# A hybrid attention encoder layer on one core: the projection's work on ScalarE and VectorE in another order, and GpSimd for part of the weight sums

## The reference, cut to what matters

```
h = rmsnorm(x, g_norm_mix)
qa, ka, va, qb, kb, vb = split(h @ w_in)
qb, kb = partial_rope(qb), partial_rope(kb)       # first 16 of 64 values of a head
oa = neighbourhood_attention(qa, ka, va, rpb); ob = windowed_gqa_sink(qb, kb, vb, sink)
x = x + concat(rmsnorm(oa), rmsnorm(ob)) @ w_out
x = x + (silu(n @ w_gate) * (n @ w_up)) @ w_down   # n = rmsnorm(x)
return rmsnorm(x, g_final)
```

## Time and profile before

| | us |
|---|---|
| median of 3 runs (lowest, highest) | 2266.8 (2265.73, 2267.71) |
| the profiled execution's own time | 2267.85 |
| its span, first to last instruction | 2266.0 |
| values phase, 12.1 to 146.7 | 134.6 |
| products, 146.7 to 462.2 | 315.5 |
| last product to the seventeenth score | 36.9 |
| the rest (attention, mix, FFN) | 1766.9 |

### The profile page before, as it was taken

The page is one execution under the profiler, slowest core; times in us unless marked ns, Lnnn a source line. Parts: engine busy times, 40 slices in busy tenths (PEclk is TensorE's granted clock), DMA queues, the critical chain, the costliest instruction groups (busy, mean ns, idle before and its releaser), DMA issues.

```text
span 2266.0 us, 33068 instructions
## 1 busy us (share of the span) xinstructions
PE 2166.6 (96%) x11168; PEld 1787.7 (79%) x11168; DVE 1565.9 (69%) x2892; ACT 1012.7 (45%) x1967; POOL 243.7 (11%) x275
## 2 busy tenths in 40 slices
PE   7888988969999999999999999999999999999998
PEld 5677766758888888888888888888888888888887
DVE  5466676649988868777666666866666678665676
ACT  5443443448889944344333334433333334131333
POOL 2234100036400000001211111100000000000000
PEclk9989998989999999999999999999999999999999
DMA  6666676899985356665555557623232276353544
GB/s 196 186 192 196 194 243 225 276 246 259 243 219 172 110 190 211 241 219 171 190 172 190 172 190 251 222 89 121 89 121 89 103 287 235 112 181 110 178 152 157
DMA packets 267558, 419.34 MB, mean 185 GB/s; under 512 B 15242, under 2 KB 157074, under 8 KB 260896
## 3 DMA queue, kind: packets, MB, share of 16 engines
q1 hardware_dynamic: 254736, 378.20, 52.2%
q0 software_dynamic: 10240, 30.48, 4.5%
q10 hardware_dynamic: 2448, 8.91, 1.3%
HBM read 264.70 MB, written 156.04 MB: 186 GB/s over the span
## 4 chain that ended last, share of the span: by engine, by line
PE 80%; DVE 7%; DMA 5%; issue 3%; ACT 3%; SPq 1%; DVEq 0%; ACTq 0%
PE late_psum L2334 11%; PE late_psum L2336 11%; PE late_psum L2335 11%; PE late_psum L2360 6%; PE late_psum L2361 6%; PE late_psum L2362 6%; PE late_psum L1278 4%; PE late_psum L1255 3%; PE late_psum L1676 3%; PE late_psum L1678 3%; PE late_psum L1677 3%; PE late_psum L853 2%; PE late_psum L855 2%; PE late_psum L854 2%; PE late_psum L1243 2%
## 5 line engine op out<-in xcount | busy, mean ns | idle before, releaser
L2334 PE MATMUL late_psum<-ff_h,ff_ring 128*128 128x512 f32 x1232 | 479.6, 389 | 1.3 <-DVE ff_acts L2195 1.2
L2336 PE MATMUL late_psum<-ff_h,ff_ring 128*128 128x512 f32 x1232 | 479.3, 389 | 0.0
L2335 PE MATMUL late_psum<-ff_h,ff_ring 128*128 128x512 f32 x1232 | 479.3, 389 | 0.0
L2334 PEld LDWEIGHTS late_psum<-ff_h,ff_ring 128*128 128x128 f32 x1232 | 231.2, 188 | 50.1 <-DVE ff_acts L2195 2.1
L2335 PEld LDWEIGHTS late_psum<-ff_h,ff_ring 128*128 128x128 f32 x1232 | 231.2, 188 | 48.0
L2336 PEld LDWEIGHTS late_psum<-ff_h,ff_ring 128*128 128x128 f32 x1232 | 231.2, 188 | 47.9
L2360 PE MATMUL late_psum<-ff_d,ff_a 128*128 128x512 f32 x616 | 240.1, 390 | 2.1 <-DVE ff_x L2253 1.4
L2362 PE MATMUL late_psum<-ff_d,ff_a 128*128 128x512 f32 x616 | 239.7, 389 | 0.0
L2361 PE MATMUL late_psum<-ff_d,ff_a 128*128 128x512 f32 x616 | 239.7, 389 | 0.0
L2253 DVE TENSOR_TENSOR ff_x<-late_psum,ff_x 128x512 f32<-128x512 f32 x224 | 153.3, 689 | 118.1 <-PE late_psum L2362 117.5
L2153 DVE TENSOR_TENSOR ff_ring<-ff_raw,ff_ring 128x512 fp32r<-128x512 f32 x176 | 130.1, 740 | 101.2 <-ACT ff_ring L2030 101.2
(11 more groups left out here) (204 smaller groups left out, 4125.8 us busy)
## 6 DMA issues: line engine op xcount, KB each, us to landing
acts_scratch<-ff_acts SPq DMA_DIRECT2D x22, 1792.0 KB, 7.5
ff_a<-acts_scratch SPq DMA_DIRECT2D x24, 960.0 KB, 5.3
ff_raw<-in_w_gate SPq DMA_DIRECT2D x44, 512.0 KB, 3.8
ff_raw<-in_w_up SPq DMA_DIRECT2D x44, 512.0 KB, 3.9
att_q_stack<-qk_scratch SPq DMA_DIRECT2D x64, 256.0 KB, 6.5
ff_d<-down_scratch SPq DMA_DIRECT2D x21, 768.0 KB, 6.8
...
```

The lines of the kernel that those rows point to most:

```text
L2334: pe.matmul(out_bank, whi[:, k], hhi[:, :, k], start=(k == 0 and not onto), stop=False, skip_group_check=onto)
L2335: pe.matmul(out_bank, whi[:, k], hlo[:, :, k], start=False, stop=False, skip_group_check=onto)
L2336: last = pe.matmul(out_bank, wlo[:, k], hhi[:, :, k], start=False, stop=(k == 3), skip_group_check=onto)
```

## The change

ScalarE and VectorE do the projection's work in another order, in both stages. In the values phase `root` is divided into `square` and `root`, `normed_tile` into `mean_tile` and `normed_tile`; the norm of tile t + 3 comes first in an iteration, square and mean of tile t + 4 last. The store of the sums is divided into four with two semaphores. In a step of the products ScalarE does the ring and the splits ahead of the results, VectorE the results of the step before and the ropes ahead of the ring; results and ropes come one or two steps later. The first runs' splits and pairs move into the values phase. The rope tables have three buffers for each half of the tokens, of which only the fourth turn reuses one. ScalarE issues the loads of the operands 2 to 6 of the second half and that of the fourth rope table. The w_out blocks have spacing 5 from step 53. GpSimd makes the weight sums of runs 6 to 13. SP's first loads of attention come at steps 91, 93 and 94, the masks of the later rows at step 97, the rest after the last result; ScalarE waits for the last stage's store (`last_stage_stored`) before the first probabilities are copied. The diff, cut:

```diff
@@ -163,9 +163,13 @@
-    OP_LOADS.update({PER_G * HALF_GROUPS - PER_G + o - 1: o for o in range(2, SEVEN)})
-    SPLIT_AT_TILE = {13: (0, 2), 14: (0, 3), 15: (0, 4)}
-    SPLIT_AT = {0: (0, 6), 24: (1, 1), 31: (1, 0), 45: (1, 2), 46: (1, 3), 47: (1, 4), 49: (1, 5), 51: (1, 6)}
+    LATE_OPS, OP_SLOTS = PER_G * HALF_GROUPS - PER_G - 2, range(2, SEVEN)
+    SPLIT_AT_TILE = {12: (0, 2), 13: (0, 3), 14: (0, 4), 15: (0, 6)}
+    PAIR_AT_TILE = {11: 0, 12: 1, 13: 2}
+    SPLIT_AT = {26: (1, 1), 33: (1, 0), 46: (1, 2), 48: (1, 3), 49: (1, 4), 51: (1, 5), 52: (1, 6)}
+    SUMS_BY_POOL, SUMS_AT = range(6, G), {1: 2}
+    PAIRS_AT = {n: (n + RING,) for n in range(PRODUCTS - RING)}
+    PAIRS_AT.update({0: (4, 5, 6), 1: (), 2: (), 3: (7,), 4: (8, 9), 5: (10, 11)})
...
     def place(n):
...
-    HI_AT = {ROPED: (2, 5, 6, 8), VALUES: (1, 6, 5, 9)}
-    ROPE_AT = (1, 4, 5, 7)
+    HI_AT = {ROPED: (3, 6, 7, 9), VALUES: (3, 7, 6, 9)}
+    ROPE_AT = (2, 5, 6, 8)
+    ROPE_SLOT = (0, 1, 2, 0)
...
-    order = sorted(((PER_G * g + HI_AT.get(kind_of(g), (1, 4, 5, 6))[i], g, i) for g in range(G) for i in range(4)))
+    order = sorted(((PER_G * g + HI_AT.get(kind_of(g), (3, 5, 6, 7))[i], g, i) for g in range(G) for i in range(4)))
...
     def is_value(g, i):
@@ -256,8 +261,14 @@
     def results_split(eng):
...
-    def near_arrived(eng):
-        eng.wait_ge(near_in, 16 * len(near_parts))
+    def last_stage_stored(eng):
+        eng.wait_ge(stored[2], max(v for r, v in stored_by.items() if r % STAGES == 2))
+    def near_arrived(eng, kind):
+        if kind == 0:
+            eng.wait_ge(near_in, 48)
+        else:
+            eng.wait_ge(near_masks_in, 32)
...
     def out_weights_stored(eng):
@@ -278,34 +289,41 @@
     def store_sums(u):
+        sp.wait_ge(h_copied, 2 * u + 2)
+        sp.dma_start(sums_dram[5, :, u - 4], hs[:, 5]).then_inc(parts_stored, 16)
...
-        sp.dma_start(sums_dram[:, :, u - 4].rearrange("o p c -> p o c"), hs[:]).then_inc(h_stored, 16)
-    def load_rope(b, turn):
-        for side, half in enumerate((0, 1) if turn == 0 else (1, 0)):
-            if turn == 0 and b == 0:
-                sp.wait_ge(v_done, NT)
-            elif turn == 0:
-                sp.wait_ge(prod_done, PER_G * HALF_GROUPS)
-            else:
-                sp.wait_ge(roped, 4 * b + side + 1)
-            cols = slice((2 * b + half) * BANK, (2 * b + half + 1) * BANK)
-            sp.dma_start(mem.p_rope[b][:, side], rope_in_dram[side].rearrange("c p s -> p c s")[:, :, cols]) \
-                .then_inc(rope_in[side], 16)
-    def load_op(o):
-        if o == 1:
-            sp.wait_ge(h_stored, 64)
-        elif o == 0:
-            sp.wait_ge(v_done, NT)
-            sp.wait_ge(h_stored, 64)
-            sp.wait_ge(roped, 4)
-            sp.wait_ge(v_turned, 2)
+        sp.dma_start(sums_dram[2:5, :, u - 4].rearrange("o p c -> p o c"), hs[:, 2:5]).then_inc(h_stored, 16)
+        sp.dma_start(sums_dram[6, :, u - 4], hs[:, 6]).then_inc(h_stored, 16)
+    def store_parts(u):
+        sp.wait_ge(h_copied, 2 * u + 1)
+        sp.dma_start(sums_dram[0:2, :, u - 4].rearrange("o p c -> p o c"), hs[:, 0:2]).then_inc(parts_stored, 16)
+    def load_rope(eng, b, i):
+        side, half = SIDES[i]
+        if i == 3:
+            eng.wait_ge(roped, 4 * b + 1)
+        elif b == 0:
+            eng.wait_ge(v_done, NT)
...
-            sp.wait_ge(prod_done, HOME_FREED[o])
-        sp.dma_start(hc[:, o, 1].bitcast(F32), sums_dram[o].rearrange("p q c -> p (q c)")).then_inc(h_in[o], 16)
+            eng.wait_ge(prod_done, PER_G * HALF_GROUPS)
+        cols = slice((2 * b + half) * BANK, (2 * b + half + 1) * BANK)
+        eng.dma_start(mem.p_rope[b][ROPE_SLOT[i]][:], rope_in_dram[side].rearrange("c p s -> p c s")[:, :, cols]) \
+            .then_inc(rope_in[1 if ROPE_SLOT[i] else 0], 16)
+    def load_op(eng, o):
+        if o < 2:
+            eng.wait_ge(parts_stored, 128)
+            eng.wait_ge(h_stored, 128)
+        if o == 0:
+            eng.wait_ge(v_done, NT)
+            eng.wait_ge(roped, 4)
+            eng.wait_ge(v_turned, 2)
+        elif o >= 2:
+            eng.wait_ge(prod_done, HOME_FREED[o])
+        eng.dma_start(hc[:, o, 1].bitcast(F32), sums_dram[o].rearrange("p q c -> p (q c)")).then_inc(h_in[o], 16)
...
     def store_result(r, g, i):
@@ -347,32 +365,32 @@
-    OUT_AT = {59 + 4 * k: k for k in range(KT)}
+    OUT_AT = {53 + 5 * k: k for k in range(KT)}
...
     def load_near(part):
...
-        sp.dma_start(dst, src).then_inc(near_in, 16)
-    def first_loads(att):
-        sp.wait_ge(prod_done, PRODUCTS - 6)
-        for slot in range(STAGES):
-            sp.wait_ge(stored[slot], max(v for r, v in stored_by.items() if r % STAGES == slot and order[r][1] < G - 2))
-        att.load_q(att.near, 0, 0)
-        sp.wait_ge(prod_done, PRODUCTS - 4)
-        att.load_k(att.near, 0, 0)
-        att.load_k(att.near, 0, 1)
-        sp.wait_ge(prod_done, PRODUCTS - 3)
-        for half in range(2):
-            sp.wait_ge(v_stored[half], 32 * NT)
-            sp.wait_ge(v_stored_by_pool[half], 32 * NT)
-        att.load_v(att.near, 0, 0)
-        att.load_v(att.near, 0, 1)
+        sp.dma_start(dst, src).then_inc(near_in if part < 3 else near_masks_in, 16)
+    def first_loads(att, turn):
+        sp.wait_ge(prod_done, PRODUCTS - SEVEN + (1, 3, 4)[turn])
+        if turn == 0:
+            for slot in range(STAGES):
+                sp.wait_ge(stored[slot], max(v for r, v in stored_by.items() if r % STAGES == slot and order[r][1] < G - 2))
+            att.load_q(att.near, 0, 0)
+        if turn == 1:
+            att.load_k(att.near, 0, 0)
+            att.load_k(att.near, 0, 1)
+        if turn == 2:
+            for half in range(2):
+                sp.wait_ge(v_stored[half], 32 * NT)
+                sp.wait_ge(v_stored_by_pool[half], 32 * NT)
+            att.load_v(att.near, 0, 0)
+            att.load_v(att.near, 0, 1)
+    def later_loads(att):
...
-    def later_loads(att):
@@ -387,39 +405,63 @@
         for t in range(NT):
...
-            if 7 <= t < NT - 1 and t % 2:
-                store_sums((t + 1) // 2)
-        load_rope(0, 0)
+            if 6 <= t < NT - 2:
+                (store_sums if t % 2 else store_parts)((t + 2) // 2)
         for n in range(LAST_STEP + 1):
-            if n == 7 * ROPED + 6:
-                load_rope(0, 1)
-            if n == PER_G * HALF_GROUPS:
-                load_rope(1, 0)
-            if n == PER_G * HALF_GROUPS + 7 * ROPED + 6:
-                load_rope(1, 1)
+            if n == 3:
+                for i in range(3):
+                    load_rope(sp, 0, i)
+            if n == PER_G * HALF_GROUPS + 3:
+                for i in range(3):
+                    load_rope(sp, 1, i)
...
-                load_op(OP_LOADS[n])
+                load_op(sp, OP_LOADS[n])
...
-            if n - 3 in OUT_AT:
-                store_out_weights(OUT_AT[n - 3])
+            if n - 2 in OUT_AT:
+                store_out_weights(OUT_AT[n - 2])
...
-                for part in range(3):
-                    load_near(part)
+                load_near(0)
+            if n in (83, 87):
+                load_near({83: 1, 87: 2}[n])
+            for r, g, i in results_at(n - 1):
+                store_result(r, g, i)
...
+                first_loads(att, 0)
+            if n == 93:
+                first_loads(att, 1)
+            if n == 94:
+                first_loads(att, 2)
+            if n == 97:
...
-            for r, g, i in results_at(n):
-                store_result(r, g, i)
-            if n == 95:
-                first_loads(att)
...
+    def first_weight_sums(eng, g):
+        r = raw[g % 2]
+        a11, a21, a22 = r[:, 0:4, 0:P], r[:, 0:4, P:2 * P], r[:, 4:8, P:2 * P]
+        eng.wait_ge(raw_in[g % 2], 16 * (g // 2 + 1))
+        if g >= 1:
+            eng.wait_ge(w_lo_done, PER_G * g - 1)
+        eng.tensor_tensor(sums[:, 0], a21, a22, ALU.add).then_inc(sums_made, 1)
+        eng.wait_ge(sums_made, 4 * g + 1)
+        eng.tensor_tensor(sums[:, 1], sums[:, 0], a11, ALU.subtract).then_inc(sums_made, 1)
+    def middle_weight_sum(eng, g):
+        a11, a21 = raw[g % 2][:, 0:4, 0:P], raw[g % 2][:, 0:4, P:2 * P]
+        eng.tensor_tensor(a21, a11, a21, ALU.subtract).then_inc(sums_made, 1)
+    def last_weight_sum(eng, g):
+        eng.wait_ge(sums_made, 4 * g + 2)
+        eng.wait_ge(w_lo_done, PER_G * g + 3)
+        eng.tensor_tensor(sums[:, 1], raw[g % 2][:, 4:8, 0:P], sums[:, 1], ALU.subtract).then_inc(sums_made, 1)
...
     def load_raw(g):
@@ -460,8 +502,15 @@
+            if g - 1 in SUMS_BY_POOL:
+                last_weight_sum(pool, g - 1)
+            if g in SUMS_BY_POOL:
+                first_weight_sums(pool, g)
+                middle_weight_sum(pool, g)
...
+        if G - 1 in SUMS_BY_POOL:
+            last_weight_sum(pool, G - 1)
...
     def load_x(t):
@@ -484,16 +533,17 @@
-                act.wait_ge(h_stored, 16 * (u - 4))
```

(101 more changed lines are left out.)

50 lines of the change are left out of this document (21 added, 29 removed).

## The result

The changed kernel took 2211.29 us in the median of 4 runs (2205.4 to 2214.93), the kernel before 2266.27 beside it; the ratio is 0.9755, 95% interval 0.9732 to 0.9777. The forecast was 2205, with 2182 to 2237 as the range. Its execution for the profile took 2212.51 us with a span of 2210.7, 55.3 us less than the profiled one of before (2267.85). Where those 55.3 us lie is read from four windows, cut where the stages of before are cut: values phase, products, start of attention up to the seventeenth score, and the rest. Columns as there: busy us and instructions of PE, PEld, DVE, ACT and POOL, then the clock, the DMA share and GB/s.

What follows compares the result with a forecast made beforehand. TensorE was taken to be busy but with waits and a lower clock in values phase and products; gains of 22.1, 32.7 and 7 us (start of attention) sum to 61.8, from 2267.85 to 2206.05, median 2205, range 2182 to 2237.

Steps and rivals of the forecast that it cites:

- DMA-bound values phase: Rival, values phase: at DMA share 0.96 transfers, not the norm, set tiles 8 to 15; values give 11, total 2216; chance 0.15.
- (a): Start of the products: the one ring-slot wait, 1.95 us, goes; pair 7 moving to step 3 gains or loses nothing.
- (b): Rope turns in the products: with three table buffers loaded at once, TensorE's waits behind late tables shrink by 12.8 us.
- (c): Products: ScalarE's waits for w_out cause 6.7 us; spacing 5 instead of 4 steps leaves 2, a gain of 4.7 us.
- (d): Products, second half: 6.5 us of waits for split operands; ScalarE issuing the loads leaves 1.8, a gain of 4.7 us.
- (e): Products: with joins first and results a step later, TensorE's 2.1 us of waits on a join go.
- (f): Products, eight runs: GpSimd's weight sums relieve VectorE but stretch its operations; net cost 3 us, bounds -2 and +10.
- Clock: Products: two thirds of the 14.1 us lost to the lower clock come back, 9.4 us (0 to 14.1).
- VectorE as the new bound: Rival, products: port conflicts, ropes and splits make joins late in runs 6 to 13; products give 20, total 2218; chance 0.13.
- slower: Rival, products: GpSimd's serial chain of sums becomes the period; at 6.8 us a sum 73 us lost, 2278; chance 0.03.
- Start of attention: After the products: earlier key loads put the first score some 2.5 us after the end, not 12; gain 7 us (0 to 12).
- the head start is eaten: Rival, start of attention: masks and second queries use up the early loads' gain; 0 there, total 2212; chance 0.10.

## Why the prediction was right, and where its terms were off

The forecast (2205, the largest chance on a gain of 62 us) held in direction and range, and the waits that it named went, but for those on w_out. That the sum came so near is in part luck: two errors of some 8 us, in the values phase and in the products, cancel. Its terms by the profiled executions:

**Values phase: 22.1 forecast, 30.0 measured.** The waits for x_normed fell by 16.0 us (16.7 forecast). The two others were too cautious. The clock gave back 14 us or so and not two thirds of 15.6: with no holes left it is 1.00 over the whole phase. And the 5 us for crowded transfers did not come: the share was 0.83 between 62 and 88 us and 0.79 from there to the end of the phase, where the working had 0.96, and TensorE waited for nothing. The rival "DMA-bound values phase" is out. The working put the waits for the store "below" those for the norm and gave them no price of their own. By the runs each of the two parts alone brings 10 us and both 28.8: the store's division was as much of the gain as the norm's order, and the working had it as a cost of 5.

**Products: 32.7 forecast, 24.4 measured.**
(a) Start: the wait of 1.95 us before product 2 went, but one of 1.70 stands before product 6, "issue" in the view. Just before it VectorE had stood 6.92 us and ScalarE 3.18 for the next raw weights, until 131.29, and product 6 starts at 134.62, right behind the work that they had put off. "Nothing needs it before product 4's join" was too hopeful; no run separates this term.
(b) Rope: both waits went, and putting them back cost 16 us. The term of 12.8 was right or a little small.
(c) w_out: this is the step that failed. "Spacing 5 instead of 4 steps takes most; I leave 2 us." Spacing sets how often a block comes, not how long before its use it is loaded. That the loads come "about three steps, 8 us, before use" was wrong as well: the split stands two steps, 5.4 us, after the load in the program, SP's queue had eaten all but 1.7 us of that at the place shown, and the transfer took 11.4 us. The waits behind ScalarE are 9.5 us, not 2. Two further steps of lead brought 10.6 us in the total. Nor did removing the rope waits merely uncover this one: put back, they stand beside it.
(d) Operands: 6.5 fell to 2.6 us (before products 53 to 55), 3.9 against 4.7 forecast. The reason given, that ScalarE issues the loads, fell: with SP as issuer the waits are no longer. The Trainium skill ("DMA: Bandwidth & Descriptors", Issuing engines are not separate DMA queues) gives another issuer no more than the issuing engine's own time; the run agrees, with 1.59 + 0.44 us of waits with SP as issuer against 0.60 + 1.59 + 0.42.
(e) Joins: the three waits of 2.1 us went, and one of 2.5 us stands before product 83. It went when w_out came later, and one of 0.8 us stands before product 90, so most of it was ScalarE's delay handed on.
(f) GpSimd's sums: a loss of 3 us forecast, a gain of about 3 measured, and none once ScalarE was in time. The bounds of -2 and +10 hold it within the scatter. The stretched operations were there (0.69 to 1.79 us at most), but VectorE had room for them. The Trainium skill ("SBUF — State Buffer", Who interferes with whom) has VectorE's operations with two inputs in SBUF contend with GpSimd's reads, for ports that one of the two holds for a whole instruction. The trace agrees: 17 of 18 stretched operations end 0.55 us after a sum of GpSimd's, and none with an input in PSUM is stretched. But a sum that nothing of VectorE's meets costs nothing: the 32 sums took 52.7 us in all, and VectorE lost 12.6 us by them: its busy time is 201.6 us without GpSimd's sums and 195.0 with them, where 19.2 were shed. The prediction's bounds for the net, a gain of 2.4 us a run and a loss of 2.8, enclose it: the gain was 0.8 us a run.
Clock: 9.4 forecast. Over the floor of 268.4 stand 16.3 us of waits and 6.4 of lower clock, where there were 14.1: 7.7 won. With w_out in time the products took 277.6 us, 5 under the forecast's 283. The rivals of this stage, "VectorE as the new bound" and "slower", are out: VectorE's part of the waits is 2.5 + 2.2 us, the longest of GpSimd's sums took 3.2 us, and by the prediction's estimate a run lengthens from 4.5 a sum on.

**Start of attention: 7 forecast, 0.9 measured in the first profile,** 3 to 6 us in the pair of kernels that differ in it alone. The first score, forecast some 2.5 us after the last product, came after 5.9: SP began the keys 8.5 us before the end of the last product and not 10.9, behind queries and stores, and their eight issues took 5.54 us, 0.69 each and not 0.46. The text warned that second queries and third keys come behind the last stores. What it missed is the other order on the same queue: the last results' stores come behind ten bulk loads, and ScalarE needs a stage free to finish (8.82 us; none with the border as before, 4.5 with the values' loads a step later). That is the rival "the head start is eaten", through the stores and not the masks, and its 2212 is the nearest to the 2211.29 measured, with values that came 8 us better and products 8 us worse than its sum.

The net: values +7.9, products -8.3, border -6.1 and -0.2 in the rest make the 6.5 us between 61.8 and 55.3 (with 0.2 us won ahead of the values phase).
